# Larger weight transfers in a mixture-of-experts kernel: a ring filled in units of four slots instead of two

## What is computed

```python
def expert_block(args):
    xb, e = args
    g = xb @ w_gate[e] + b_gate[e]
    u = xb @ w_up[e] + b_up[e]
    g = jnp.minimum(g, SWIGLU_LIMIT)
    u = jnp.clip(u, -SWIGLU_LIMIT, SWIGLU_LIMIT)
    glu = g * jax.nn.sigmoid(SWIGLU_ALPHA * g)
    return ((u + 1.0) * glu) @ w_down[e] + b_down[e]
```

## Time and profile before

| | |
|---|---|
| time, median of 3 runs | 1146.5 us (1146.3, 1146.5 and 1892.33) |
| the profiled execution | 1146.93 us, of which the span is 1145.1 us |
| TensorE busy | 1072.0 us (94% of the span) |
| mean granted TensorE clock | 0.984 |
| bytes moved | 438.15 MB, mean 383 GB/s |
| share of 16 DMA engines' time, main queue | 90.2% |
| on the chain that ended last | PE 73%, DMA 22% |

### The profile page before, as it was taken

How to read it: one execution, slowest core, us unless ns; L and a number is a source line. 1 busy time by engine, 2 the same in 40 slices (tenths; PEclk the granted TensorE clock), 3 DMA queues, 4 the chain that set the end, 5 groups by cost and what they waited for, 6 DMA issues and landing times.

```text
span 1145.1 us, 11709 instructions
## 1 busy us (share of the span) xinstructions
PE 1072.0 (94%) x5004; PEld 507.3 (44%) x5004; DVE 207.7 (18%) x471; ACT 131.7 (12%) x225; POOL 9.7 (1%) x17
## 2 busy tenths in 40 slices
PE   7999999988999899999989998999799979998997
PEld 6686888543443344343434432433243324342433
DVE  4123043122021021111120202020202020202022
ACT  1022260110001001000100000001000100010002
POOL 2000000000000000000000000000000000000000
PEclk9999999989999999999999998999999999999999
DMA  8982354569999999999999999999999999999995
GB/s 336 380 340 107 148 202 174 213 265 421 428 432 432 429 432 429 436 428 434 432 429 435 430 435 427 434 432 429 435 432 434 427 434 433 429 426 428 428 429 224
DMA packets 24349, 438.15 MB, mean 383 GB/s; under 512 B 4736, under 2 KB 6016, under 8 KB 7808
## 3 DMA queue, kind: packets, MB, share of 16 engines
q1 hardware_dynamic: 24176, 437.67, 90.2%
q10 hardware_dynamic: 144, 0.07, 0.0%
HBM read 436.28 MB, written 1.05 MB: 382 GB/s over the span
## 4 chain that ended last, share of the span: by engine, by line
PE 73%; DMA 22%; DVE 2%; ACT 1%; another core or an unknown queue 1%; issue 0%; ACTq 0%; DVEq 0%; SPq 0%
PE ps L1334 30%; DMA ring<-in_experts 22%; PE ps L1373 14%; PE ps L1073 10%; PE ps L1276 4%; PE ps L1382 3%; PE ps L1202 2%; PE ps L1061 2%; PE ps L1243 1%; PE ps L1239 1%; PE ps L1318 1%; DVE g L990 1%; DVE region_va L987 1%; PE ps L1364 1%; ACT region_va L633 1%
## 5 line engine op out<-in xcount | busy, mean ns | idle before, releaser
L1334 PE MATMUL ps<-ring,xT 128*64 128x512 f32 x2048 | 456.9, 600 | 24.7 <-DMA ring<-in_experts 24.4
L1334 PEld LDWEIGHTS ps<-ring,xT 128*64 128x64 f32 x2048 | 143.8, 138 | 312.6 <-issue 281.0
L1373 PE MATMUL ps<-ring,region_va 128*64 128x512 f32 x1024 | 230.5, 607 | 6.5 <-ACT region_va L633 4.6
L1373 PEld LDWEIGHTS ps<-ring,region_va 128*64 128x64 f32 x1024 | 83.3, 140 | 143.6 <-issue 130.7
L1073 PE MATMUL ps<-ring 128*128 128x256 f32 x512 | 115.4, 387 | 6.9 <-DMA ring<-in_head 6.9
L1073 PEld LDWEIGHTS ps<-ring 128*128 128x128 f32 x512 | 98.6, 194 | 21.6 <-DMA ring<-in_head 6.9
L971 DVE TENSOR_SCALAR g<-ps 128x1024 f32<-128x1024 f32 x16 | 19.6, 1225 | 346.4 <-PE ps L1334 346.4
L1276 PEld LDWEIGHTS ps<-sel,x 128*128 128x128 f32 x544 | 64.4, 196 | 12.8 <-issue 11.1
L1276 PE MATMUL ps<-sel,x 128*128 128x128 f32 x544 | 66.4, 281 | 1.6 <-DVE oh L921 1.6
L929 DVE TENSOR_TENSOR xT<-ps,g_ffn 128x512 f32<-128x512 f32 x34 | 23.5, 690 | 202.4 <-PE ps L1276 202.4
L1382 PE MATMUL ps<-g,g_T 128*128 128x512 f32 x128 | 59.2, 605 | 0.0
(11 more groups left out here) (190 smaller groups left out, 399.9 us busy)
## 6 DMA issues: line engine op xcount, KB each, us to landing
ring<-in_experts SPq DMA_DIRECT2D x78, 4096.0 KB, 43.7
ring<-in_experts SPq DMA_DIRECT2D x35, 2048.0 KB, 48.7
ring<-in_head SPq DMA_DIRECT2D x13, 2048.0 KB, 15.7
ring<-in_experts SPq DMA_DIRECT2D x2, 1024.0 KB, 51.7
ring<-in_head SPq DMA_DIRECT2D x2, 512.0 KB, 6.5
ring<-in_head SPq DMA_DIRECT2D x1, 1024.0 KB, 9.0
x<-in_x SPq DMA_DIRECT2D x2, 512.0 KB, 22.4
out<-x SPq DMA_DIRECT2D x4, 256.0 KB, 2.7
```

What stands on the lines that cost most here:

```text
L1334: last = mm(bank(banks + half)[rows, :], xT[:, 2 * m + c, rows], w[:, c, k, half * W512:(half + 1) * W512], start=False, stop=m == 3 and c ...
L1373: last = mm(bank(first + half)[rows, :], hTm[:, 2 * m + c, rows], w[:, c, k, half * W512:(half + 1) * W512], start=m == 0 and c == 0, stop ...
```

## The change

The unit becomes four slots: `UNITS` is 3 instead of 6, and a unit is all gate, all up or all down weights of a pair. Pairs 2 to 13 come in 8 MB transfers of rows of 64 KB, each asked for when four slots have been used. Pair 1, which came in units of two, now comes in single slots of 2 MB, asked for slot by slot, as pairs 14 and 15 did before and still do. Pair 0 comes in 2 MB transfers as before. The array of expert weights in HBM is laid out anew: rows of 64 KB where there were rows of 32 KB, so that a 2 MB slot is a quarter of each row (16 KB of 64 KB) and not a half of it.

```diff
-UNITS = LOADS_PER_PAIR // 2
+UNITS = 3
+UNIT_LOADS = LOADS_PER_PAIR // UNITS
...
         def unit(m):
-            return ring[:, 2 * m * SLOT_COLS:2 * (m + 1) * SLOT_COLS]
+            return ring[:, UNIT_LOADS * m * SLOT_COLS:UNIT_LOADS * (m + 1) * SLOT_COLS]
...
             def load_half(row, p):
 
-                m, odd = divmod(p, 2)
-                cols = slice(odd * SLOT_COLS, (odd + 1) * SLOT_COLS)
+                m, part = divmod(p, UNIT_LOADS)
+                cols = slice(part * SLOT_COLS, (part + 1) * SLOT_COLS)
                 sp_.dma_start(whole(SLOT_OF[p]), experts_v[row][:, cols]
-                              ).then_inc(unit_loaded[m] if odd else slot_loaded[SLOT_OF[p]], 16)
+                              ).then_inc(unit_loaded[m] if part == UNIT_LOADS - 1 else slot_loaded[SLOT_OF[p]], 16)
...
-                        if not closing:
-                            sp_.wait_ge(load_used, n * LOADS_PER_PAIR + 2 * m + 2)
+                        if not (closing or i is None):
+                            sp_.wait_ge(load_used, n * LOADS_PER_PAIR + UNIT_LOADS * (m + 1))
                             load_unit(row, m)
                             continue
-                        for p in (2 * m, 2 * m + 1):
+                        for p in range(UNIT_LOADS * m, UNIT_LOADS * (m + 1)):
                             sp_.wait_ge(load_used, n * LOADS_PER_PAIR + p + 1)
...
                     def loaded(m):
 
                         s = SLOT_OF[m]
-                        if m % 2 == 0 and (first_pair or closing):
+                        if m % UNIT_LOADS < UNIT_LOADS - 1 and (opening or closing):
                             before = len(range(s, HEAD_LOADS, HEAD_RING)) if s < HEAD_RING else 0
-                            pe.wait_ge(slot_loaded[s], (before + (1 if first_pair else 2 + q)) * 16)
+                            pe.wait_ge(slot_loaded[s], (before + (1 if opening else 3) + q) * 16)
                         elif last_pair and m == LOADS_PER_PAIR - 1:
                             pe.wait_ge(last_rows, 16)
                         else:
-                            pe.wait_ge(unit_loaded[m // 2], (n + 1) * 16)
+                            pe.wait_ge(unit_loaded[m // UNIT_LOADS], (n + 1) * 16)
...
-    out = np.empty((PAIRS, 3, 2, P, 4, 2, D), np.float32)
+    out = np.empty((PAIRS, UNITS, P, KC, 2, D), np.float32)
     for w, name in enumerate(("w_gate", "w_up", "w_down")):
-        out[:, w] = a[name].reshape(PAIRS, 2, 2, 4, P, D).transpose(0, 2, 4, 3, 1, 5)
-    return out.reshape(PAIRS * UNITS * P, 2 * SLOT_COLS)
+        out[:, w] = a[name].reshape(PAIRS, 2, KC, P, D).transpose(0, 3, 2, 1, 4)
+    return out.reshape(PAIRS * UNITS * P, UNIT_LOADS * SLOT_COLS)
```

More of the change, by code:

```diff
@@ L402, in load_last @@
                     cols = slice(c * (SLOT_COLS // 2), (c + 1) * (SLOT_COLS // 2))
-                    from_cols = slice((2 + c) * (SLOT_COLS // 2), (3 + c) * (SLOT_COLS // 2))
+                    from_cols = slice((2 * UNIT_LOADS - 2 + c) * (SLOT_COLS // 2), (2 * UNIT_LOADS - 1 + c) * (SLOT_COLS // 2))
                     sp_.dma_start(whole(SLOT_OF[p])[:, cols], experts_v[row][:, from_cols]).then_inc(loaded, 16)
@@ L429, in _ @@
                 sp_.wait_ge(*slot_free[SLOT_OF[p]])
-                load_half(p // 2, p)
+                load_half(p // UNIT_LOADS, p)
             sp_.wait_ge(rt_done, 2)
```

## The result

The changed kernel takes 1150.41 us in the median of 8 runs, the kernel before 1146.4. The ratio is 1.0035, 95% interval 1.0025 to 1.0044: 4 us slower, well inside the 2% that the forecast gave to "no change", and 0.7 us from the forecast number. The lines of the two fences that follow answer to the earlier trace rows. First the page of the changed kernel: the GB/s of the 40 slices, and the chain by engine.

A forecast was written before the change was run, and what follows sets the result against it. The DMA queue was taken to bound the kernel. Stream 3.3 us late (earlier pair 1, hole, start-up, longer rows), TensorE 4.6 late and deciding: span +4.6, median 1151.1 us; 1147 to 1157 held over 8 in 10.

The forecast's parts named there:

- no change: Whole kernel: a time within 2% of the kernel before, 23 us either way; chance 0.95.
- The bound: Load stream after 250 us: the queue never idles, so any delay or shortening reaches the end one for one.
- Part 1, the rows: Pairs 2 to 13: 64 KB rows save 0.074 us per 8 MB unit, 19.36 us each, 2.7 us less over 36.
- the rival of slow pieces: Pairs 14 and 15: 16 KB pieces spread over 64 KB rows load slowly; at +1.6 us each, 1190 us; chance 0.03.
- Part 2, the hole: Before pair 2: queue empty 306.8 to 313.8 us, 7 us, plus 5.0 start-up; stream 3.3 us late in all.
- Part 3, the lump: Pair 13's last four slots land together at 1015.8; TensorE becomes the later, ending pair 15's up at 1119.1, +4.6 us.
- the queue's own bound: End of pair 15's up matmuls if loads alone decided: 1117.3 us, 1.8 us before TensorE's 1119.1.
- Serial cost for each transfer: Rival for all queued loads: each pays a 2.3 us start-up, so fewer transfers bring the end near 1082; chance 0.01.
- The clock: Rival in even pairs: after 5 us waits TensorE's two slots take 8.78 instead of 7.09; 1152.8 us; chance 0.07.

The follow-up runs named there:

- the run with short pieces: The changed kernel with the old HBM layout, rows of 32 KB, so each 8 MB transfer has two 32 KB pieces a partition; 1152.19 us, ratio 1.0046.
- the run whose added wait was always met: The changed kernel plus a SyncE wait before pair 2's first 8 MB unit, meant to enlarge the hole but miscounted, so without effect; 1149.79 us, ratio 1.0028.

## Why the prediction was right

**The bound.** That a delay of the stream comes out at the end is shown in both directions: taking the hole away gave 7.5 us, and adding 15.5 to it cost 14.7.

**Part 1, the rows.** 19.36 a unit was forecast, 19.35 measured, and the run with short pieces at 19.43 shows the cause. 16 KB pieces at 64 KB distance come at 428 GB/s, the same as at 32 KB, so the rival of slow pieces has nothing for it, and the rule of the Trainium skill ("DMA: Bandwidth & Descriptors", Latency and other measured facts), which reports losses from 512 KiB, is neither shown nor contradicted at this distance. The other figure that the prediction takes from that page of the Trainium skill, 2.0 us fixed (Anatomy of one DMA), stands in a section on transfers issued from GpSimd, and the weight loads here are issued from SyncE; 2 us for each transfer in series is not what these traces show for them either.

**Part 2, the hole.** The place and the size were right (6.7 us for 7.0), but that the landing agrees to 0.1 us is luck: two of its terms were off by 1.1 and cancelled. (Pair 1 was in at 308.2 and not 306.8; that changes the idle time and not the landing.) The ask came at 314.9 and not 313.8, 0.7 of it since pair 1's gate matmuls ended later in this execution, the rest since the ask follows TensorE by 0.6 (the entry of the loop included) where I had put 0.2. The start-up of the 8 MB transfer was 23.2 - 19.35 = 3.9 and not 5.0: it did not grow from 4 MB. Together the first unit landed at 338.1 for 338.2. The last was in at 1015.7 for 1015.8. The 3.9 is one execution's: the same transfer took 21.8 to 22.3 us to land in three other runs. What follows it hardly moves with that. Counted back by 31 units of 19.35 from TensorE's wait before up in pair 12 (938.33 and 938.50), the first unit of the stream belongs at 338.4 in the changed kernel's trace and at 338.6 in that of the run whose added wait was always met, where it landed at 336.9. By this count the start-up is 4.2.

**Part 3, the lump.** TensorE's times were right step by step: 1033.78 for 1034.0, 1090.88 for 1090.2, 1119.78 for 1119.1. But I called it a price of 1.8 us, the difference to the queue's own bound, and that was mis-sized: smaller transfers that let TensorE keep up cost the queue as much. In the sum nothing changes, since only the end of up was added.

One more step of this part agrees without being what happened. The prediction lets the last big unit, at 1015.8, release TensorE. The chain that ended last (start, length, what) goes through the unit before it, pair 13's up, which lands at 996.35, and through no load after that:

```profile
954.69 41.66 DMA ring<-in_experts
996.39 7.09 PE ps L1335 x32
...
1015.10 0.59 ACT region_va L634
1015.70 0.14 issue
1015.83 13.95 PE ps L1374 x64
```

Up, gather and transposes take TensorE 19.4 us, as long as the queue takes for a unit, so TensorE is ready for the down weights just when they land; ScalarE's last piece is what it waits for, and the 0.3 us of that wait stand in the trace of the kernel before too. By these times either lump alone, that of the up weights or that of the down weights, would have held TensorE back to the same point.

**The rivals.** Serial cost for each transfer is excluded by the unit spacing of 19.35 and by the single slots at 428 GB/s. The clock did fall, 0.984 to 0.973, and did not carry the loss: TensorE had slack in those pairs, and the kernel with pairs 2 and 3 in single slots has 0.976 and is 3.2 us faster than before. Where TensorE sets the end, though, the clock counts. The trace of the run whose added wait was always met, which is the changed kernel once more, has pair 14 and the gate of pair 15 so:

```profile
1066.92 15.23 PE L1375 MATMUL ps<-ring,region_va 128*64 128x512 f32 x64
...
1089.71 13.96 PE L1336 MATMUL ps<-ring,xT 128*64 128x512 f32 x64
```

Its mean granted clock from 1065 to 1084 us is 0.91, that of the changed kernel's trace 0.83. The gate of pair 15 begins at 1089.71 and not at 1090.88, though the down stage of pair 13 began 0.17 later (1016.00 for 1015.83), and the span is 1148.9 and not 1149.9. So the step-by-step agreement of part 3 is with one execution, 1.25 over the median. That the median lies 0.7 under the forecast is likely this microsecond of TensorE's clock in pair 14.

What remains unsettled is about a microsecond in each of two places: pair 1 lands 1.4 later than the sum, and with pairs 2 and 3 in single slots the units of pairs 4 to 13 take 1.6 more than 30 spacings. No run separates the pauses behind this.

## What to carry to other kernels

Where a queue of transfers is the bound, look at the moment at which it runs dry and at the ask that ends it, not at the share of busy time or at the waits of the engine that consumes: here TensorE was busy all through the hole and the price came 800 us later, undiminished. A larger unit is asked for later, because it waits for more memory to come free; make the unit fine where the consumer is close behind the queue, and large once enough is under way. The longer rows were worth 0.08 us a unit, 2.9 us in 36, which a single hole of 7 us outweighs. The fastest kernels of this case have both, fine units up to pair 2 or 3 and 8 MB units behind them: 1143 to 1144 us, against 1148.55 with fine units throughout.

## What the runs showed of the hardware

The spacing of queued transfers from SyncE follows the number of pieces very regularly: 4.895 us for 2 MB in 16 KB rows, 9.716 for 4 MB in 32 KB rows, 19.43 for 8 MB in two 32 KB pieces a partition, 19.35 for 8 MB in 64 KB rows. For 8 MB these are 19.58, 19.43, 19.43 and 19.35 us with 512, 256, 256 and 128 pieces in 4, 2, 1 and 1 transfers: about 0.08 us for each 128 pieces, and nothing that the number of transfers adds. A 64 KB row travels as one packet (the count of packets above).

A transfer into an idle queue lands later than one spacing: by 2.3 us for 2 MB; by 3.8 for 4 MB and 2.4 in the run with the kernel before and pair 1 in single slots (12.1 us from 307.75 on); by 3.9 for 8 MB in two runs (23.2 us), 2.4 in two others (21.8) and 2.9 in the run with pair 1 in units of two (22.3). The size beyond 4 MB does not show in it. Counted back from later landings in four of these runs, the stream of 8 MB units starts 3.8 to 4.2 us late, whatever the first landing itself showed.
